# Regrouping four of eight MLP input tiles by 32x32 block transposes and DRAM instead of transposing them on TensorE

## The chip, the core and the metric

One NeuronCore of a Trainium2 chip runs the whole layer. The metric is the device time of one execution in microseconds; the median of several runs is given. The engines work side by side, each through its own instructions in order: PE (TensorE), ACT (ScalarE), DVE (VectorE), POOL (GpSimd, here a DMA queue and a few elementwise operations) and SP (a DMA queue). They wait for each other at semaphores.

## What is computed

One layer of a streaming encoder on x of 1024 tokens by 1024 channels, in float32. A token-mixing part runs three branches (windowed attention, a state-space layer, cross-attention), gates and merges them; what follows it is the part that matters here:

```python
x = x + rmsnorm(merged @ w_out, g_mix_post)
h = rmsnorm(x, g_mlp_pre)
f = square(relu(h @ w_up)) @ w_down        # w_up 1024x4096, w_down 4096x1024
x = x + rmsnorm(f, g_mlp_post)
```

Tokens are cut into eight tiles of 128. The kernel keeps float32 accuracy by splitting every operand of a product into a high part (float32r, made by ScalarE) and a low part (the rest, made by VectorE) and adding three products: high-high, high-low and low-high.

## The kernel before, in words

The stage around the change goes through the eight tiles in an order written out by hand, `OUT_ORDER` (L50): `w0 w1 w2 h0 w3 h1 w4 h2 w5 h3 w6 h4 w7 h5`, and then `h6 h7` between the first MLP products. A `w` is the output projection of a tile, an `h` the turning of a tile of the MLP input h from tokens-by-channels into channels-by-tokens, the layout that the MLP's products need. All engines walk through the same order. For a tile t:

- TensorE, `w_out` (L2442): 24 matmuls of 512 columns into each of two banks, through the helper at L2146. For tiles 0 and 1 these are laid out differently, ahead of the loop.
- ScalarE copies both banks into `acc[t]` (L889), squares them and sums (`square_o`, L1145), and does the same for the residual of the tile before (`square_x`).
- VectorE, `residual` (L1826): scales the projection by the gain (L1831), makes 1/sqrt of the mean square in eight small steps (`rstd`, L1357 to L1363), multiplies and adds x (L1835). Then `h2` of the tile before (L1838): rstd again, and L1844 writes the normalised tile into one of two slots of `tok`. From the third tile on it first waits until TensorE has turned the tile that had the slot.
- TensorE, `h2_transposes` (L2450): eight 128x128 transposes (L2156) of a slot into two banks. ScalarE's `h2_hi` (L1150) takes the high part from the banks into `hThi` (L1154), VectorE's `h2_lo` (L1847) the low part into `hTlo` (L1852).
- POOL (loop at L808): waits for the residual of the tile, stores it (x1, L810), waits until the store has landed and h2 has been made, and loads x of the tile after the next (`x_load`, L798). There are two slots for x, `yx`.

Before the first MLP product TensorE waits until the parts of tiles 0 to 3 have been taken out of the banks, and in `plain_mlp`, before the fifth product, for those of tiles 4 to 7. The first product also needs the split weights of its unit; VectorE makes their low parts (`prep_lo`, L388) at the step `w7`, behind `h4`. Each `w` and each `h` takes the next two of the eight banks, in the order of `OUT_ORDER` (`out_event`, L134).

The kernel turns other things by blocks already: in the attention branches VectorE transposes 128x1024 tiles in 32x32 blocks (L1520, L1601), POOL stores the blocks to DRAM and brings them back regrouped with four loads of 128 KB per tile (L686, L713).

Of the kernel before, what the change touches and what calls it, by code (L numbers as in the profile page):

```python
# [16 lines left out]
P = 128  # L17
D = 1024
L = 1024
# [28 lines left out]
          ("glu", 16), ("mergeM", 16), ("mergeS", 16), ("out", 28), ("upA", 4), ("mlp", 192)]  # L48

OUT_ORDER = ["w0", "w1", "w2", "h0", "w3", "h1", "w4", "h2", "w5", "h3", "w6", "h4", "w7", "h5", "h6", "h7"]  # L50
FIRST = {}
_n = 0
for _name, _count in STAGES:
# [80 lines left out]
def out_event(kind, t, e):  # L134
    if kind == "h" and t > 5:
        return FIRST["upA"] + 2 + 3 * (t - 6) + e
    return FIRST["out"] + 2 * OUT_ORDER.index(f"{kind}{t}") + e

# [10 lines left out]
def hybrid_layer(nc, a, out):  # L149
# [4 lines left out]
    with ctx:  # L154
# [101 lines left out]

        craw = yst2.rearrange("p h (r d x) -> p h r d x", r=RP, d=2)
        x_blocks = [t1, t2]
        blocks = pT[:, :, :, :].rearrange("p a b c -> p a (b c)")
        prob_of = lambda q: prob[:, 2 * q:2 * q + 2, :].rearrange("p e c -> p (e c)")  # L260
        y_slots = [yst2[:, 0, :], yst2[:, 1, :]] + [xs[:, h, :, :].rearrange("p r n -> p (r n)") for h in range(2)]
# [21 lines left out]

        p_dram = nc.dram_tensor("prob_scratch", (16, P, L), f32, kind="Internal").ap()
        x_dram = nc.dram_tensor("x_blocks_scratch", (4, P, 2, 512), f32, kind="Internal").ap()
        y_dram = nc.dram_tensor("y_scratch", (2, BT, P, L), f32, kind="Internal").ap()
        g_dram = nc.dram_tensor("gate_scratch", (3, KT, P, L), f32, kind="Internal").ap()
        x1_dram = nc.dram_tensor("x1_scratch", (2, P, D), f32, kind="Internal").ap()
# [24 lines left out]
        turned, rope_done = sem("turned"), sem("rope_done")  # L313
        y_sent = [sem(f"y_sent{s}") for s in range(4)]
        x_turned, x_out, x_back_in = sem("x_turned"), sem("x_out"), sem("x_back_in")
        blocks_turned, blocks_out, p_back = sem("blocks_turned"), [sem(f"blocks_out{s}") for s in range(2)], sem("p_back")
        g_sent = [sem(f"g_sent{s}") for s in range(2)]
        gate_in = [sem(f"gate_in{s}") for s in range(4)]
# [331 lines left out]
        def _(pool):  # L650
# [157 lines left out]
            for t in range(NT):  # L808
                pool.wait_ge(x1_made, t + 1)
                g.dma_start(x1_dram[t - tile_of(NT - 2)] if tile_of(t) > 5 else out_rows[t], yx[:, t % 2, :]).then_inc(x1_sent, 16)  # L810
                if t + 2 < NT:
                    pool.wait_ge(x1_sent, 16 * (t + 1))
                    pool.wait_ge(h2_made, t + 1)
                    x_load(t + 2)
            g.memset(acc[:, :, :], 0.0).then_inc(acc_zero, 1)
            pool.wait_ge(h2_made, NT)
            for e in range(2):
# [65 lines left out]
        def _(act):  # L883
# [264 lines left out]
                square2("o", acc[:, t, :], 10 + t)  # L1148

            def h2_hi(t):  # L1150
                for e in range(2):
                    n = out_event("h", t, e)
                    wait_full(act, n)
                    A.activation(hThi[:, 4 * e:4 * e + 4, t * P:(t + 1) * P],  # L1154
                                 banks[n % 8][:, :].rearrange("p (k t) -> p k t", k=4), ACT.Copy).then_inc(split_hi, 1)
# [182 lines left out]
        def _(dve):  # L1338
# [487 lines left out]
            def residual(t):  # L1826
                for e in range(2):
                    wait_taken(dve, out_event("w", t, e))

                scaled = acc[:, (t + 4) % NT, :]  # L1830
                mark(V.tensor_tensor(scaled, acc[:, t, :], tok[:, 0:D], mul))  # L1831
                dve.wait_ge(sq_o, t + 1)
                rstd(sumsq[:, 10 + t:11 + t])
                dve.wait_ge(x_back[t % 2], 16 * (t // 2 + 1))
                V.scalar_tensor_tensor(out=yx[:, t % 2, :], in0=scaled, scalar=stat[:, 1:2], in1=yx[:, t % 2, :], op0=mul, op1=add)\  # L1835
                    .then_inc(x1_made, 1)

            def h2(t):  # L1838
                dve.wait_ge(sq_x, t + 1)
                if t >= 2:  # L1840
                    wait_full(dve, out_event("h", t - 2, 0))
                    wait_full(dve, out_event("h", t - 2, 1))
                rstd(sumsq[:, 18 + t:19 + t])
                V.scalar_tensor_tensor(out=tok[:, (2 + t % 2) * D:(3 + t % 2) * D], in0=yx[:, t % 2, :], scalar=stat[:, 1:2],  # L1844
                                       in1=tok[:, D:2 * D], op0=mul, op1=mul).then_inc(h2_made, 1)

            def h2_lo(t):  # L1847
                for e in range(2):
                    n = out_event("h", t, e)
                    sl = (slice(None), slice(4 * e, 4 * e + 4), slice(t * P, (t + 1) * P))  # L1850
# [286 lines left out]
        def _(pe):  # L2137
# [317 lines left out]

            for step in OUT_ORDER[:-2]:
                t = int(step[1])
                if step[0] == "h":
                    h2_transposes(t)
                    continue  # L2460
                for e in range(2 if t > 1 else 0):
                    w_out(t, e)

            for t in range(4):
                for e in range(2):
                    wait_taken(pe, out_event("h", t, e))


            def plain_mlp():
                for pc, (s, cc, hf) in enumerate(UP_FIRST):  # L2470
# [1 line left out]
                    if pc in (2, 3):  # L2472
                        h2_transposes(pc + 4)
                    if pc == 4:
                        for t in range(4, NT):
                            for e in range(2):
                                wait_taken(pe, out_event("h", t, e))
                    unit(u)
# [109 lines left out]
```

## Time and profile before

| | us |
|---|---|
| median of three runs | 1439.28 |
| lowest and highest run | 1438.74, 1439.55 |
| the profiled execution | 1438.89 |
| its span, first to last instruction | 1436.9 |
| TensorE busy in the span | 1422.6 (99%) |
| VectorE busy | 1047.4 (73%) |
| ScalarE busy | 514.9 (36%) |
| POOL busy | 241.7 (17%) |

The profile is one execution on the chip. A row of a timeline gives the start in us from the beginning of the span, the duration in us, the engine, the line of the kernel, the operation, what it writes and reads, and in brackets how long the engine had been idle and what released it. Matmuls are pipelined, so that their durations overlap; the distance of their starts is their pace. For a DMA the duration is that of its issue, and the time to landing runs from the issue to the semaphore that tells that the data is there.

### The profile page before, as it was taken

The page shows a single profiled execution, that of the slowest core. Times are in us where ns is not written, and L with a number is a line of the kernel's source. Part 1 is how long each engine was busy: PE and PEld are TensorE (multiplying, and loading weights), DVE is VectorE, ACT ScalarE, POOL GpSimd, SP SyncE. Part 2 cuts the span into 40 slices and gives each one's busy share as a digit, 9 for nine tenths or more (in the row PEclk, how much of TensorE's full clock was granted, in tenths as well). Part 3 has the DMA queues.
Part 4 walks back from the last instruction along what each step waited for, and adds up shares of the span by engine and source line. Part 5 has one row for each costly group of instructions (what it writes and reads, how often), then busy time and mean ns, then how long its engine had stood idle before and what let it go on. Part 6 is the DMA issues. An engine that isn't in the chain of part 4 may idle for free.

```text
span 1436.9 us, 18375 instructions
## 1 busy us (share of the span) xinstructions
PE 1422.6 (99%) x6998; PEld 1178.1 (82%) x6998; DVE 1047.4 (73%) x1718; ACT 514.9 (36%) x637; POOL 241.7 (17%) x392
## 2 busy tenths in 40 slices
PE   8999999999999999999999999999999999999997
PEld 7888688878888888888888888888888888888886
DVE  6769768964854526456766779797979796979887
ACT  4445653131211352311333432333334333434334
POOL 0003313431111131001000304211010102020112
PEclk9999999999999999999999999999999999999999
DMA  9306525954234387234433447936363737364546
GB/s 337 74 30 190 166 85 175 275 195 149 71 106 139 93 272 256 93 96 151 162 104 89 133 146 228 299 118 203 119 203 117 234 94 239 105 203 143 160 152 117
DMA packets 136241, 227.04 MB, mean 158 GB/s; under 512 B 23048, under 2 KB 74288, under 8 KB 136176
## 3 DMA queue, kind: packets, MB, share of 16 engines
q0 software_dynamic: 52960, 139.24, 31.2%
q1 hardware_dynamic: 83200, 86.92, 19.1%
q8 instruction: 42, 0.69, 0.2%
q14 instruction: 23, 0.19, 0.0%
q10 hardware_dynamic: 16, 0.00, 0.0%
HBM read 175.53 MB, written 50.59 MB: 157 GB/s over the span
## 4 chain that ended last, share of the span: by engine, by line
PE 94%; DVE 3%; DMA 1%; issue 1%; ACT 0%; DVEq 0%; SPq 0%; ACTq 0%
PE bank L2146 55%; PE bank L2515 17%; PE bank L2535 15%; PE bank L2186 1%; PE bank L2156 1%; PE bank L2248 1%; PE bank L2268 1%; DMA raw<-in_w_down_dram 1%; PE bank L2375 1%; PE bank L2380 1%; PE bank L2284 1%; PE bank L2345 1%; PE bank L2330 1%; DMA xst<-in_mem_dram 0%; DVE wlo L388 0%
## 5 line engine op out<-in xcount | busy, mean ns | idle before, releaser
L2146 PE MATMUL bank<-hThi,whi 128*128 128x512 f32 x800 | 313.9, 392 | 0.1
L2146 PE MATMUL bank<-hThi,wlo 128*128 128x512 f32 x800 | 311.4, 389 | 0.0
L2146 PE MATMUL bank<-hTlo,whi 128*128 128x512 f32 x800 | 311.4, 389 | 0.0
L2146 PEld LDWEIGHTS bank<-hThi,whi 128*128 128x128 f32 x800 | 150.2, 188 | 32.2 <-issue 1.2
L2146 PEld LDWEIGHTS bank<-hThi,wlo 128*128 128x128 f32 x800 | 150.2, 188 | 31.6
L2146 PEld LDWEIGHTS bank<-hTlo,whi 128*128 128x128 f32 x800 | 150.2, 188 | 30.7
L1212 ACT ACTIVATE whi<-raw 128x1024 fp32r<-128x1024 f32 x91 | 95.3, 1055 | 182.3 <-DVE raw L1953 97.6
L1943 DVE TENSOR_TENSOR wlo<-raw,whi 128x1024 fp32r<-128x1024 f32 x91 | 110.9, 1219 | 34.4 <-ACT whi L1212 34.4
L2535 PE MATMUL bank<-whi,yhi 128*128 128x512 f32 x336 | 130.8, 389 | 0.6 <-DVE acc L1976 0.6
L2535 PE MATMUL bank<-wlo,yhi 128*128 128x512 f32 x336 | 130.7, 389 | 0.0
L2515 PE MATMUL bank<-hThi,whi 128*128 128x512 f32 x336 | 130.7, 389 | 0.0
L2515 PE MATMUL bank<-hTlo,whi 128*128 128x512 f32 x336 | 130.7, 389 | 0.0
L2515 PE MATMUL bank<-hThi,wlo 128*128 128x512 f32 x336 | 130.7, 389 | 0.0
L2535 PE MATMUL bank<-whi,ylo 128*128 128x512 f32 x336 | 130.7, 389 | 0.0
L388 DVE TENSOR_TENSOR wlo<-raw,whi 128x2048 fp32r<-128x2048 f32 x33 | 75.2, 2280 | 57.4 <-ACT whi L382 57.1
L382 ACT ACTIVATE whi<-raw 128x2048 fp32r<-128x2048 f32 x32 | 61.1, 1911 | 79.7 <-PE bank L2146 51.8
L1019 ACT ACTIVATE scr<-bank 128x512 f32<-128x512 f32 x48 | 28.5, 597 | 162.9 <-PE bank L2146 133.6
L1976 DVE TENSOR_TENSOR acc<-bank,acc 128x1024 f32<-128x1024 f32 x72 | 86.0, 1217 | 1.0 <-PE bank L2535 1.0
L2535 PEld LDWEIGHTS bank<-whi,yhi 128*128 128x128 f32 x336 | 63.1, 188 | 14.0 <-DVE acc L1976 1.0
L2535 PEld LDWEIGHTS bank<-whi,ylo 128*128 128x128 f32 x336 | 63.1, 188 | 13.2
L2515 PEld LDWEIGHTS bank<-hThi,wlo 128*128 128x128 f32 x336 | 63.1, 188 | 13.2
L2515 PEld LDWEIGHTS bank<-hThi,whi 128*128 128x128 f32 x336 | 63.1, 188 | 13.1
(398 smaller groups left out, 2568.7 us busy)
## 6 DMA issues: line engine op xcount, KB each, us to landing
hThi<-h_scratch POOLq DMA_DIRECT2D x42, 512.0 KB, 4.8
hTlo<-h_scratch POOLq DMA_DIRECT2D x42, 512.0 KB, 5.7
raw<-in_w_in_dram SPq DMA_DIRECT2D x34, 512.0 KB, 7.2
raw<-in_w_up_dram SPq DMA_DIRECT2D x32, 512.0 KB, 4.3
raw<-in_w_down_dram SPq DMA_DIRECT2D x32, 512.0 KB, 4.6
gate_scratch<-scr POOLq DMA_DIRECT2D x48, 256.0 KB, 3.1
tok<-gate_scratch POOLq DMA_DIRECT2D x24, 512.0 KB, 4.2
prob_scratch<-pT POOLq DMA_DIRECT2D x16, 512.0 KB, 3.5
```

Source lines behind the costliest of these rows:

```text
L382: nc.scalar.activation(parts(u)[0], raw[:, u % 2, :], ACT.Copy).then_inc(w_hi, 1)
L388: nc.vector.tensor_tensor(lo, raw[:, u % 2, :], hi.bitcast(f32), sub).then_inc(w_lo, 1)
L1019: A.activation(scr[:, gp % 2, :], banks[n % 8][:, :], ACT.Sigmoid).then_inc(bank_free[n % 8], 1)
L1212: A.activation(w_slot(whi, place), source, ACT.Copy).then_inc(w_hi, 1)
L1943: V.tensor_tensor(w_slot(wlo, place), source, w_slot(whi, place).bitcast(f32), sub).then_inc(w_lo, 1)
L1976: V.tensor_tensor(dst[:, 2 * h:2 * h + 2, :], pair_banks(k), dst[:, 2 * h:2 * h + 2, :], add).then_inc(pair_free[k], 1)
L2146: ins = T.matmul(dst, lhs(k)[p], rhs(k)[q], start=start and k == 0 and i == 0, stop=stop and k == kt - 1 and i == 2)
L2156: ins = T.transpose(banks[n % 8][:, i * P:i * P + P] if dsts is None else dsts[i], src, by)
L2186: ins = T.matmul(banks[n % 8][:, 0:256], wk[:, c] if s < 2 else memT[:, k, c], memT[:, k, :] if s < 2 else wk, start=k == 0, stop=k == KT - 1)
L2248: ins = T.matmul(banks[n % 8][:, hh * 256:hh * 256 + 256], tokq[:, h, (e // 2) * P:(e // 2 + 1) * P], kmT[:, h, :], start=True, stop=True)
L2515: ins = T.matmul(banks[2 * k + c][:, :], w[:, kk, c * P:c * P + P], x[:, kk, :], start=opens and kk == 0 and i == 0, stop=kk == 3 and i == ...
L2535: ins = T.matmul(banks[2 * k + t % 2][:, :], x[:, kk, rows], w[:, kk, :], start=opens and kk == 0 and i == 0, stop=kk == 1 and i == 2, ski ...
```

## The change

For tiles 0 to 3 (`HB = 4`) TensorE no longer transposes h. VectorE, behind `h2`, transposes the slot in 32x32 blocks into `acc[t]`. POOL, at the end of its turn for that tile, waits for this, stores the blocks to a new DRAM tensor, waits for the store to land, and brings them back with four loads into the same slot of `tok`. ScalarE waits for these loads and makes the high parts out of the slot, with a rearranged reading order, VectorE the low parts. `h2` of tiles 2 to 5 waits for VectorE's own low parts instead of TensorE's transposes, the residual of tiles 4 to 7 for the landing of a block store, since it writes where the blocks lay. The four `h` steps leave the sequence of banks. Before the first MLP product TensorE waits for eight counts of the new semaphore `h_parts`. Tiles 4 to 7 are as before. The core of the diff:

```diff
-          ("glu", 16), ("mergeM", 16), ("mergeS", 16), ("out", 28), ("upA", 4), ("mlp", 192)]
+          ("glu", 16), ("mergeM", 16), ("mergeS", 16), ("out", 20), ("upA", 4), ("mlp", 192)]
...
+HB = 4
+OUT_EVENTS = [w for w in OUT_ORDER if w[0] == "w" or int(w[1]) >= HB]
...
-    return FIRST["out"] + 2 * OUT_ORDER.index(f"{kind}{t}") + e
+    return FIRST["out"] + 2 * OUT_EVENTS.index(f"{kind}{t}") + e
...
+        h2_slot = lambda t: tok[:, (2 + t % 2) * D:(3 + t % 2) * D]
...
+        hb_dram = nc.dram_tensor("h2_blocks_scratch", (HB, P, L), f32, kind="Internal").ap()
...
                     x_load(t + 2)
+                if t < HB:
+                    pool.wait_ge(blocks_turned, 16 + t + 1)
+                    g.dma_start(hb_dram[t], acc[:, t, :]).then_inc(blocks_out[t % 2], 16)
+                    pool.wait_ge(blocks_out[t % 2], 128 + 0 * (1 - t % 2) + 16 * (t // 2 + 1))
+                    src = hb_dram[t].rearrange("(a s) (b x) -> b s a x", a=4, b=4)
+                    for b in range(4):
+                        g.dma_start(h2_slot(t)[32 * b:32 * b + 32, :].rearrange("s (a x) -> s a x", a=4), src[b]).then_inc(xp_back[t % 2], 16)
...
             def h2_hi(t):
+                if t < HB:
+                    act.wait_ge(xp_back[t % 2], 16 * 16 + 64 * (t // 2 + 1))
+                    for e in range(2):
+                        A.activation(hThi[:, 4 * e:4 * e + 4, t * P:(t + 1) * P].rearrange("p k (a r) -> p k a r", a=4),
+                                     h2_slot(t).rearrange("p (a k r) -> p k a r", a=4, k=KT)[:, 4 * e:4 * e + 4], ACT.Copy).then_inc(split_hi, 1)
+                    return
...
                 scaled = acc[:, (t + 4) % NT, :]
+                if 4 <= t < HB + 4:
+                    dve.wait_ge(blocks_out[t % 2], 128 + 0 * (1 - t % 2) + 16 * (t // 2 - 1))
...
                 dve.wait_ge(sq_x, t + 1)
-                if t >= 2:
+                if 2 <= t < HB + 2:
+                    dve.wait_ge(h_parts, 2 * (t - 1))
+                elif t >= 2:
...
                                        in1=tok[:, D:2 * D], op0=mul, op1=mul).then_inc(h2_made, 1)
+                if t < HB:
+                    dve.wait_ge(h2_made, t + 1)
+                    V.transpose(acc[:, t, :].rearrange("p (b k r) -> p k b r", b=4, k=KT),
+                                h2_slot(t).rearrange("p (k b s) -> p k b s", k=KT, b=4)).then_inc(blocks_turned, 1)

             def h2_lo(t):
+                if t < HB:
+                    for e in range(2):
+                        by_block = lambda y: y[:, 4 * e:4 * e + 4, t * P:(t + 1) * P].rearrange("p k (a r) -> p k a r", a=4)
+                        dve.wait_ge(split_hi, 20 + 2 * t + e + 1)
+                        V.tensor_tensor(by_block(hTlo), h2_slot(t).rearrange("p (a k r) -> p k a r", a=4, k=KT)[:, 4 * e:4 * e + 4],
+                                        by_block(hThi).bitcast(f32), sub).then_inc(h_parts, 1)
+                    return
...
                 if step[0] == "h":
-                    h2_transposes(t)
+                    if t >= HB:
+                        h2_transposes(t)
                     continue
...
-            for t in range(4):
-                for e in range(2):
-                    wait_taken(pe, out_event("h", t, e))
+            pe.wait_ge(h_parts, 8)
```

## Rows read from the trace of the kernel before

**Rows 1.** The page, the chain that ended last, its shares by engine.

```profile
PE 94%; DVE 3%; DMA 1%; issue 1%; ACT 0%; DVEq 0%; SPq 0%; ACTq 0%
```

**Rows 2.** The chain's pieces in time (start, us), then TensorE's timeline at tiles 4 and 5.

```profile
739.72 0.87 PE bank L2156 x8
740.59 10.90 PE bank L2146 x48
...
786.65 0.60 PE L2156 MATMUL bank<-ident,tok 128*128 128x128 f32 x4
...
799.21 0.48 PE L2146 MATMUL bank<-hThi,whi 128*128 128x512 f32 x1
```

**Rows 3.** VectorE's timeline: h2, residual, rstd, residual's end, next rstd, low parts, weights.

```profile
736.72 1.28 DVE L1844 SCALAR_TENSOR_TENSOR tok<-yst,stat,tok 128x1024 f32<-128x1024 f32 x1
740.45 1.23 DVE L1831 TENSOR_TENSOR acc<-acc,tok 128x1024 f32<-128x1024 f32 x1 [2.45 <-ACT acc L889]
741.62 0.15 DVE L1357 TENSOR_SCALAR stat<-sumsq 128x1 f32<-128x1 f32 x1
...
743.40 1.28 DVE L1835 SCALAR_TENSOR_TENSOR yst<-acc,stat,yst 128x1024 f32<-128x1024 f32 x1
744.61 0.15 DVE L1357 TENSOR_SCALAR stat<-sumsq 128x1 f32<-128x1 f32 x1
...
...
794.68 1.28 DVE L1852 TENSOR_TENSOR hTlo<-bank,hThi 128x512 fp32r<-128x512 f32 x2
795.88 4.48 DVE L388 TENSOR_TENSOR wlo<-raw,whi 128x2048 fp32r<-128x2048 f32 x2
```

**Rows 4.** Line 1520, the block transpose of attention: count, ns min/median/max, first and last start.

```profile
L1520 DVE STREAM_TRANSPOSE pT<-prob x8: 1245/1246/1248, 115.2 to 149.6; 128x1024 f32<-128x1024 f32 x8
```

**Rows 5.** ScalarE's timeline, a half tile copied from SBUF.

```profile
812.27 0.63 ACT L1202 ACTIVATE yhi<-yst 128x512 fp32r<-128x512 f32 x1 [5.93 <-DVE yst L1909]
```

**Rows 6.** POOL's timeline, x loads of tiles 3 and 6 and an x1 store.

```profile
748.22 0.53 POOL L798 DMA_DIRECT2D yst<-in_x_dram  x1 [8.60 <-DVE tok L1844]
748.79 0.54 POOL L810 DMA_DIRECT2D x_scratch<-yst  x1
...
783.56 0.53 POOL L798 DMA_DIRECT2D yst<-in_x_dram  x1 [10.65 <-DVE tok L1844]
```

**Rows 7.** POOL in attention: a block store, its landing; four loads behind it, theirs.

```profile
151.19 0.56 POOL L690 DMA_DIRECT2D prob_scratch<-pT  x1 [1.56 <-DVE pT L1520]
...
DMA to landing us min/median/max: 4.8/4.8/4.8
...
156.23 2.18 POOL L686 DMA_DIRECT2D prob<-prob_scratch  x4 [2.30 <-DMA prob_scratch<-pT]
...
DMA to landing us min/median/max: 2.8/5.0/6.5
```

**Rows 8.** Line 810, the six x1 stores between 738 and 797 us, landing.

```profile
DMA to landing us min/median/max: 5.1/5.4/6.8
```

**Rows 9.** Line 810, the x1 store at 731.2 us, landing.

```profile
DMA to landing us min/median/max: 2.9/2.9/2.9
```

**Rows 10.** Landings: line 678 at 303.1 us; line 840's two stores at 850.9; line 734 at 300.9.

```profile
DMA to landing us min/median/max: 4.3/4.3/4.3
...
DMA to landing us min/median/max: 2.9/3.3/3.7
...
DMA to landing us min/median/max: 2.8/2.9/2.9
```

**Rows 11.** Line 798, the six x loads between 738 and 797 us, landing.

```profile
DMA to landing us min/median/max: 4.4/4.6/6.4
```

**Rows 12.** Two tiles of the stage: busy by engine, granted clock, DMA share, GB/s.

```profile
740.45:752.23 11.78, 11.78 (x59) 9.84 (x58) 7.85 (x24) 4.48 (x9) 1.07 (x2) 1.00 0.46 139
752.23:764.00 11.77, 11.77 (x59) 9.83 (x58) 7.84 (x23) 4.47 (x9) 1.06 (x2) 1.00 0.32 91
```

**Rows 13.** The core's span and mean granted clock.

```profile
core 0: 1436.9 us, clock 0.998
```

More of the change, by code:

```diff
@@ L315, in hybrid_layer @@
         x_turned, x_out, x_back_in = sem("x_turned"), sem("x_out"), sem("x_back_in")
+        h_parts = sem("h_parts")
         blocks_turned, blocks_out, p_back = sem("blocks_turned"), [sem(f"blocks_out{s}") for s in range(2)], sem("p_back")
@@ L2474, in plain_mlp @@
                     if pc == 4:
-                        for t in range(4, NT):
+                        if HB > 4:
+                            pe.wait_ge(h_parts, 2 * HB)
+                        for t in range(HB, NT):
                             for e in range(2):
```

## Prediction

> **What bounds the kernel now.** I read the chain that ended last first: TensorE carries 94% of it, no other engine more than 3% [rows 1]. Whatever TensorE is spared, and whatever it is made to wait, goes to the end. Then I read the stage that the diff touches, engine by engine: the output projection and the transposes of the MLP input, from 728 to 817 us. TensorE's pieces of the chain follow each other there without a gap [rows 2]: eight transposes, 0.87 us, then a tile's projection, 48 matmuls in 10.90. Four of eight tiles lose their transposes: 4 x 0.87 = **3.48 us** is all that can be gained, and TensorE's pace becomes 10.90 us a tile where it was 11.77.
>
> The sum is made against the profiled execution: 1438.89 us, a span of 1436.9 and 1.99 around it. The median of the runs is 1439.28, 0.39 above; the difference that I find is added to the median.
>
> **The change part by part.** *VectorE.* A tile now takes 1.17 + 1.78 + 1.21 us for the residual, the same 1.78 + 1.21 for h2 and 1.20 for the low parts [rows 3], 8.35 together. A block transpose of this very shape takes 1.25 [rows 4]; for its wait on the h2 just written I allow 0.1, since the 1.78 of rstd hold eight small steps that wait for each other like that. Low parts read from SBUF instead of PSUM: at the pace of elements either way, nothing. That is 9.7 us in a tile of 10.90: hidden as long as no input is late; if one is, all of it queues behind.
>
> *ScalarE* reads eight halves from SBUF, 0.63 us each [rows 5], beside TensorE: nothing. But it now waits in order until a tile is back from DRAM, with the copies of the next projection behind that wait, and VectorE's residual behind them.
>
> *TensorE* gives up its waits for those banks and gets one for the parts, and the projections have four pairs of banks to themselves: nothing.
>
> *POOL* is the place that decides. Today it issues, per tile, one load of x and one store of x1, back to back, and waits only for VectorE [rows 6]. After the change its loop runs in one line: the x1 store, **wait until it has landed**, x load, block store, **wait until it has landed**, four loads, and only then the next x1 store. (The first of these waits exists today, but the wait for h2 covers it.) So a circle of POOL is: landing of the x1 store + 0.25 + x load issue 0.53 + landing of the block store + 0.25 + four issues 2.2. The 0.25 is from landing to the next issue: a store of 151.19 lands after 4.8, at 156.0, and POOL goes on at 156.23; four loads of the shape wanted here take 2.2 to issue [rows 7].
>
> The landings: the block store stands directly behind an x load, as the x1 store does today. Six of those take 5.1 to 6.8, median 5.4 [rows 8]; the only one with nothing ahead takes 2.9 [rows 9]. I take **5.3**, between shortest and median, since the 6.8 came once. The x1 store will stand behind four loads of 128 KB, which no row shows at this size. Below: the lone store, 2.9. Above: the store behind an x load, 5.4. Between: a store of half the size directly behind four such loads took 4.3, beside other traffic, and the second of two full stores issued together 3.7 [rows 10]. I take **3.7**: the four loads leave at the pace of their issue, 0.55 us each, and so fill the queue hardly more than one store does.
>
> The circle is then 3.7 + 0.25 + 0.53 + 5.3 + 0.25 + 2.2 = **12.23 us**, more than TensorE's 10.90. What is late is the x load that the residual needs. In time: h2 of tile 0 is made at 738.0 [rows 3] and transposed at 739.35, its store starts 0.3 later at 739.65 (so long after the last transpose starts the store in rows 4 and 7), lands at 744.95, and the loads are issued from 745.2 to 747.4. There the x1 store of tile 1 starts, and a circle apart the x loads of tiles 3, 4, 5 and 6: 751.35, 763.6, 775.8 and 788.05 (today the first goes at 748.22, the last at 783.56 [rows 6]). They land after 4.6 [rows 11].
> - x of tile 5 is there at 780.4; the residual's last step, 1.21, and h2, 2.99, give h2(4) at 784.65. TensorE wants it after projection 6, whose end is now at 786.65 [rows 2] and comes 3.48 earlier, 783.15: a pause of 1.5.
> - TensorE goes on: 784.7 + 0.87 + 10.90 = 796.45. x of tile 6 is there at 792.65, h2(5) at 796.9: pause 0.45.
> - The first MLP product needs low parts of its weights, which VectorE makes in 2.24 behind h2(5) and 1.2 us of low parts [rows 3]: 796.9 + 1.2 + 2.24 + 0.1 = 800.4. Today it starts at 799.21 [rows 2].
>
> So the 3.48 us are paid back and 1.2 more: 1439.28 + 1.2 = **1440.5 us**. The blocks' own way back is just covered: if the loads land in 2.9, as a pass with nothing ahead of it did [rows 10], tile 1's parts leave VectorE waiting for x of tile 4 some 0.6 us; at the 4.0 of busier passes, which I count in the range, it costs about half a microsecond. Each 0.1 us of either landing is worth 0.4 at the end, since four circles stand one behind the other; so the ends lie far apart.
>
> **The rivals.** *A: the full gain, 1435.8 us.* If both stores land like a lone store or one behind a store (2.9 to 3.7), the circle is 9.0 to 10.6 us and fits into 10.90; nothing pauses and 3.48 us stay. For it: the DMA engines are busy 46% and 32% of a tile in this stage [rows 12]. Against it: every store behind an x load took 5.1 or more, in this very stage. The Trainium skill ("DMA: Bandwidth & Descriptors", section on the anatomy of one DMA on the gpsimd path) fits 2.0 us plus the bytes over 436 GB/s, by my estimate 3.2 us for each store; by that rule this case would come about. The lone row (2.9) agrees with it, the rows behind an x load don't.
>
> *B: slower, 1442.9 to 1446.9 us.* The x1 store behind the four loads lands in 4.3 (the half-size row) to 5.3 (like the one behind an x load): four times 0.6 to 1.6 us more than the sum has. It decides from 4.1 us on, where the time passes +0.2%. For it: the only row with that very order; against it: that row had other traffic beside it.
>
> *C: slower, about 1443.5 us.* The last of the four loads lands after 6.5 us, as in the pass of rows 7: tile 2 is back at 777.8 instead of 774.2; ScalarE's two parts and two copies (some 2.6), the residual (4.2) and h2 (3.0) then end at 787.6, 3.0 us behind the sum. Against it: nothing else uses the queues in this stage.
>
> *D: about 1443.4 us.* The granted clock is 1.00 in this stage [rows 12] and 0.998 over the span [rows 13]; no row shows what a pause in the middle does to it. All that the clock cost in this execution is 0.002 x 1436.9 = 2.9 us, and that is my price on top of the sum. The Trainium skill ("TensorE: Matmul & The Clock Gate", Part 1) has the clock fall from 2.4 to 1.2 GHz when the engine idles and rise again under work; no run here shows it in mid-kernel.
>
> That the change removes no TensorE time can be left out: the transposes stand on the chain [rows 2].
>
> **How the numbers follow.** No change that can be told (0.2%, 2.9 us, is about what a measurement of this kernel can tell): the sum and its surroundings, 0.42. A: 0.20. B 0.23, C 0.10 and D 0.05 are slower: 0.38. The range goes from A's floor to the upper part of B: 1435.5 to 1445.5. The likeliest case's own range is 1436.4 to 1442.2.
>
> **What would show it.** In the trace after: 32 transposes of h2 on TensorE instead of 64; POOL's x1 stores of tiles 1 to 4 some 12.2 us apart, the x loads of tiles 5 and 6 at about 775.8 and 788; a pause of TensorE ahead of the transposes of tile 4, released by VectorE's h2, and one ahead of the first MLP product. I am wrong if those stores are 10.9 us apart and nothing pauses (A), if a block store behind an x load lands in about 3 us, if a projection waits for banks, or if ScalarE's wait for the blocks ends later than the x load (C).

## The result, and the profile after

The changed kernel takes **1444.05 us** (median of 7 runs, 1442.63 to 1447.91) against 1439.28 for the kernel before beside it (7 runs, 1438.11 to 1440.51): a ratio of 1.0037, 95% interval 1.0025 to 1.0049. It is slower by 4.8 us where the prediction had 1.2: inside its range, above the likeliest case's own (1436.4 to 1442.2). The profiled execution took 1444.53 us, with a span 5.7 us longer than that of [rows 13].

The core's span and clock, then the waits of TensorE in the changed kernel: engine, tile and line, what was waited for; us in total, times, longest.

```profile
core 0: 1442.6 us, clock 0.997
...
PE bank L2189 <- DVE tok L1866: 2.9, 2, 2.6
PE bank L2179 <- issue: 2.4, 1, 2.4
PE bank L2549 <- DMA hTlo<-h_scratch: 1.8, 1, 1.8
```

The first two are new and stand in the stage that was changed; the third stands 115 us later, in the MLP. The chain of the page no longer helps: its shares (below, to be read beside [rows 1]) add up to 38%, so it does not reach back to the stage.

```profile
PE 35%; DMA 1%; DVE 1%; POOL 1%; issue 0%; ACT 0%; DVEq 0%; POOLq 0%
```

POOL's timeline in the stage, the turns of tiles 1 to 4, to be read beside [rows 6]: start, us, line, what is issued, and in brackets the idle time before it.

```profile
747.25 0.57 POOL L815 DMA_DIRECT2D out_dram<-yst  x1
751.06 0.56 POOL L803 DMA_DIRECT2D yst<-in_x_dram  x1 [3.24 <-DMA out_dram<-yst]
751.61 0.53 POOL L822 DMA_DIRECT2D h_blocks_scratch<-acc  x1
758.62 2.22 POOL L826 DMA_DIRECT2D tok<-h_blocks_scratch  x4 [6.48 <-DMA h_blocks_scratch<-acc]
760.83 0.56 POOL L815 DMA_DIRECT2D x_scratch<-yst  x1
765.57 0.56 POOL L803 DMA_DIRECT2D yst<-in_x_dram  x1 [4.17 <-issue]
766.12 0.53 POOL L822 DMA_DIRECT2D h_blocks_scratch<-acc  x1
771.55 2.22 POOL L826 DMA_DIRECT2D tok<-h_blocks_scratch  x4 [4.89 <-DMA h_blocks_scratch<-acc]
773.76 0.56 POOL L815 DMA_DIRECT2D x_scratch<-yst  x1
777.46 0.56 POOL L803 DMA_DIRECT2D yst<-in_x_dram  x1 [3.13 <-DMA x_scratch<-yst]
778.01 0.53 POOL L822 DMA_DIRECT2D h_blocks_scratch<-acc  x1
783.59 2.22 POOL L826 DMA_DIRECT2D tok<-h_blocks_scratch  x4 [5.04 <-DMA h_blocks_scratch<-acc]
785.80 0.56 POOL L815 DMA_DIRECT2D out_dram<-yst  x1
789.57 0.56 POOL L803 DMA_DIRECT2D yst<-in_x_dram  x1 [3.21 <-DMA out_dram<-yst]
```

The turn is the line of work that was foretold. From x1 store to x1 store it takes 13.58, 12.93 and 12.04 us (forecast 12.23), and the x loads leave at 751.06, 765.57, 777.46 and 789.57 (forecast 751.35, 763.6, 775.8 and 788.05). Two of the turns are long for reasons of their own: the block store of tile 1 landed after 6.7 us, and in the next turn POOL sat 4.17 us where the store of x1 had landed after 3.5.

Landings of the x1 stores of tiles 1 to 4, of the block stores, of the four loads, and of the x loads in this stage, to be read beside [rows 7, 8, 10, 11].

```profile
DMA to landing us min/median/max: 3.4/3.5/3.5
...
DMA to landing us min/median/max: 4.6/5.2/6.7
...
DMA to landing us min/median/max: 2.8/2.9/3.0
...
DMA to landing us min/median/max: 4.3/4.6/6.0
```

VectorE's steps that TensorE waits for, the last the low parts of the MLP's first weights, with the block transpose of the same profile [rows 3, 4], then ScalarE's copies from the slots, grouped [rows 5].

```profile
L1870 DVE STREAM_TRANSPOSE acc<-tok x4: 1245/1246/1247, 738.6 to 774.4; 128x1024 f32<-128x1024 f32 x4
...
782.10 1.29 DVE L1855 SCALAR_TENSOR_TENSOR yst<-acc,stat,yst 128x1024 f32<-128x1024 f32 x1 [0.89 <-DMA yst<-in_x_dram]
785.08 1.28 DVE L1866 SCALAR_TENSOR_TENSOR tok<-yst,stat,tok 128x1024 f32<-128x1024 f32 x1
...
799.74 4.48 DVE L393 TENSOR_TENSOR wlo<-raw,whi 128x2048 fp32r<-128x2048 f32 x2
...
L1166 ACT ACTIVATE hThi<-tok 128x512 fp32r<-128x512 f32 x8 | 4.6, 624 | 31.0 <-DMA tok<-h_blocks_scratch 31.0
```

The residual of tile 5 waits for its x, and h2(4) comes out at 786.3 instead of 784.65. TensorE's timeline at the three pauses shows it, to be read beside [rows 2]:

```profile
786.41 1.09 PE L2189 MATMUL bank<-ident,tok 128*128 128x128 f32 x8 [2.64 <-DVE tok L1866]
...
798.68 1.09 PE L2189 MATMUL bank<-ident,tok 128*128 128x128 f32 x8 [0.23 <-DVE tok L1866]
...
802.12 0.77 PE L2179 MATMUL bank<-hThi,whi 128*128 128x512 f32 x1 [2.35 <-issue]
```

TensorE stood 2.64, 0.23 and 2.35 us: 5.22, where 3.48 had been taken from it (32 transposes of h2 are left in the stage, where the kernel before has 64). The profile gives no releaser for the third pause; it ends when the first half of the weights' low parts is made, at 799.74 + 2.24. And the first MLP product, at 802.12, takes 0.77 for its first matmul where [rows 2] have 0.48. Busy time by engine, granted clock (0.50 is 1.2 GHz, 1.00 is 2.4 GHz), DMA share and GB/s there, to be read beside [rows 12]:

```profile
786.00:788.00 2.00, 1.59 (x11) 1.50 (x12) 0.36 (x1) 0.00 (x0) 0.36 (x1) 1.00 0.93 307
802.00:804.00 2.00, 1.88 (x5) 1.52 (x6) 2.00 (x2) 0.51 (x2) 0.00 (x0) 0.50 0.96 378
804.00:806.00 2.00, 2.00 (x7) 1.58 (x6) 1.90 (x7) 0.00 (x0) 0.00 (x0) 0.66 1.00 350
```

The clock stayed up behind the pause of 2.64 us and fell behind that of 2.35. The 5.7 us of the span then divide at three marks. TensorE would have begun the transposes of tile 4 at 786.41 - 2.64 = 783.77 without the pause; in the execution before it was 786.65, or 783.17 less the 3.48. So 0.6 us are older than any pause. Up to the first product, 12.56 us in the execution before, it now takes 802.12 - 783.77 = 18.35: 5.8 us, the pauses of 5.22 and some tenths in which the engine runs dry and fills again. From there to the end it is 640.5 us where it was 637.7: 1.2 of these 2.8 are the longer wait in the MLP (1.8 us where there was one of 0.6), and **1.6** are left for the clock. -3.48 + 0.6 + 5.8 + 1.2 + 1.6 = 5.7.

### The profile page after: what moved, and what is told of

It is laid out like the page before. It is cut to its first block and busy times, and to the rows that moved or that the text cites. A ratio compares the mean times of both kernels' runs of the same rounds, so it can differ in the third digit from the quotient of the medians.

```text
span 1442.6 us, 18327 instructions
## 1 busy us (share of the span) xinstructions
PE 1421.9 (99%) x6966; PEld 1176.0 (82%) x6966; DVE 1053.2 (73%) x1722; ACT 514.6 (36%) x637; POOL 253.0 (18%) x412
## 5 line engine op out<-in xcount | busy, mean ns | idle before, releaser
L2569 PEld LDWEIGHTS bank<-whi,ylo 128*128 128x128 f32 x336 | 63.1, 188 | 13.1
L2549 PEld LDWEIGHTS bank<-hThi,wlo 128*128 128x128 f32 x336 | 63.1, 188 | 13.1
```

The source lines that it names most:

```text
L2549: ins = T.matmul(banks[2 * k + c][:, :], w[:, kk, c * P:c * P + P], x[:, kk, :], start=opens and kk == 0 and i == 0, stop=kk == 3 and i == ...
L2569: ins = T.matmul(banks[2 * k + t % 2][:, :], x[:, kk, rows], w[:, kk, :], start=opens and kk == 0 and i == 0, stop=kk == 1 and i == 2, ski ...
```

## The experiments

The theory: POOL's turn is what puts the loads of x late, and so makes the pauses; the clock and the later wait come on top. The kernel before was run beside each of three groups of kernels, each group on one chip: 1439.15 us beside the store first, the x loads on SP and the first row of runs with TensorE kept awake; 1439.59 beside the blocks on SP, the dose, the first repetition of the change and the six tiles; 1439.54 beside the doubled dose, the second repetition and the second row with TensorE kept awake.

### The turn made shorter

**The block store ahead of the wait for the x1 store.** The two landings then run side by side.

```diff
+                if t < HB:
+                    pool.wait_ge(blocks_turned, 16 + t + 1)
+                    g.dma_start(hb_dram[t], acc[:, t, :]).then_inc(blocks_out[t % 2], 16)
                 if t + 2 < NT:
                     pool.wait_ge(x1_sent, 16 * (t + 1))
                     pool.wait_ge(h2_made, t + 1)
                     x_load(t + 2)
                 if t < HB:
-                    pool.wait_ge(blocks_turned, 16 + t + 1)
-                    g.dma_start(hb_dram[t], acc[:, t, :]).then_inc(blocks_out[t % 2], 16)
                     pool.wait_ge(blocks_out[t % 2], 128 + 0 * (1 - t % 2) + 16 * (t // 2 + 1))
```

> POOL issues the block store ahead of the x load instead of behind it; everything else is as in the changed kernel. Theory P (POOL's circle of two in-line waits makes the x loads late): the block store now stands behind the x1 store alone and lands in some 3.5 to 3.7 us instead of 5.1 to 6.7, both waits overlap, the circle falls from about 12.9 us to 7 to 10, the x loads follow VectorE again, TensorE's pause ahead of the transposes of tile 4 (2.6 us) and ahead of the first MLP product (2.35) shrink to 1 us or less together, and the clock stays at 1.00: 1435.8 to 1437.5 us. Rival S (the blocks' round trip in front of ScalarE's in-order wait ends last): the trip is only 1 to 2 us shorter, the copies of the projections still wait behind it, pauses of 2 us or more stay: 1440 to 1443.

Measured: 1439.98 us, ratio 1.0003 (0.9994 to 1.0012): between the theory and the rival, and nearer to the rival's number. The x loads leave at 751.42, 763.44, 774.53 and 785.35, the last 4.2 us earlier than with the change, and the pauses shrink to 0.82 and 1.03 us. Order alone gives back some 4 us, and the granted clock is 1.00 from 783 to 808. Why the pauses do not go altogether is in POOL's rows; the landings of the four block stores stand behind them:

```profile
773.98 0.56 POOL L818 DMA_DIRECT2D h_blocks_scratch<-acc  x1 [5.12 <-DVE acc L1871]
774.53 0.54 POOL L803 DMA_DIRECT2D yst<-in_x_dram  x1
...
DMA to landing us min/median/max: 2.9/2.9/3.9
```

The x load now stands behind the block store, and with it behind the wait for VectorE's block transpose: the x1 store of this turn had landed at 772.3 (768.31 and 4.0), and the x load left at 774.53. VectorE still waited for x last, 1.1 to 2.5 us in each of tiles 4 to 6, and not for ScalarE, as the rival had it. The block store took 2.9 us, with the x load issued behind it instead of ahead of it.

**The x loads on SP's queue**, which has nothing to do in this stage; POOL is left with the x1 store and the way of the blocks.

```diff
+            yx_sp = yst[:, :, :].rearrange("p (s a) c -> p s (a c)", s=2)
...
+                if s == 1:
+                    for t in range(NT - 2):
+                        sp.wait_ge(x1_sent, 16 * (t + 1))
+                        sp.wait_ge(h2_made, t + 1)
+                        sp.dma_start(yx_sp[:, t % 2, :], x[t + 2]).then_inc(s_in[t % 2], 16)
...
-                if t + 2 < NT:
+                if t >= HB and t + 2 < NT:
                     pool.wait_ge(x1_sent, 16 * (t + 1))
-                    pool.wait_ge(h2_made, t + 1)
-                    x_load(t + 2)
...
-                dve.wait_ge(x_back[t % 2], 16 * (t // 2 + 1))
+                dve.wait_ge((x_back if t < 2 else s_in)[t % 2], 16 * (t // 2 + 1))
```

> The x loads of tiles 2 to 7 are issued by SP's queue with the same waits; POOL keeps the x1 stores and the blocks. Theory P: POOL's circle loses the x load and the wait for the x1 store (x1 store issue 0.56, block store landing 3.7 to 5.3, 0.25, four issues 2.2: 7 to 8.5 us, below TensorE's 10.9), x is there in time, no pause above 1 us, 1435.8 to 1437.5 us. Rival S: the blocks come back no earlier relative to h2, ScalarE's wait stays, 1440 to 1443.

Measured: 1437.53 us, ratio 0.9992 (0.998 to 1.0004), an interval that still holds 1. No pause is left in the stage: the first product starts at 795.80, 3.41 us before that of [rows 2], which is the saving. From there on 2.38 us go into one wait for the MLP's loads, as in the changed kernel:

```profile
912.00 0.50 PE L2553 MATMUL bank<-hThi,whi 128*128 128x512 f32 x1 [2.38 <-DMA hTlo<-h_scratch]
```

**The blocks on SP's queue instead**, x loads and x1 stores on POOL as before the change.

```diff
+                if s == 1:
+                    for t in range(HB):
+                        sp.wait_ge(blocks_turned, 16 + t + 1)
+                        sp.dma_start(hb_dram[t], acc[:, t, :]).then_inc(s_in[t % 2], 16)
+                        sp.wait_ge(s_in[t % 2], 16 + 16 * (t // 2 + 1))
+                        back = hb_dram[t].rearrange("(a s) (b x) -> b s a x", a=4, b=4)
+                        for b in range(4):
+                            sp.dma_start(tok[32 * b:32 * b + 32, (2 + t % 2) * D:(3 + t % 2) * D].rearrange("s (a x) -> s a x", a=4), back[b]).then_inc(s_in[2 + t % 2], 16)
...
-                if t < HB:
-                    pool.wait_ge(blocks_turned, 16 + t + 1)
...
```

> The block stores and the four loads of each tile go out on SP's queue (other semaphores, nothing else changed), so POOL's turn is again x1 store, its landing, x load. Theory (POOL's circle is what puts the loads of x late): x loads 10.9 to 11.0 us apart, no pause of TensorE over 0.5 us in the stage, the first product at 795.5 to 796.5 us after the start, 1435.5 to 1438 us. Rival (the transfers themselves are in each other's way, 16 DMA engines for all queues): x1 stores and x loads land as late as with the change, pauses of 1 us or more stay, 1440 us or more. A third (SP's queue brings the blocks back later, since each of its four loads is issued behind the other and the weights' loads stand behind them): ACT waits over 10 us for a tile, and the pause is ahead of the first product.

Measured: **1436.54 us, ratio 0.9979 (0.9971 to 0.9988)**: faster than the kernel before by 3.05 of the 3.48 us. SP's queue and POOL's in the stage:

```profile
749.92 0.34 SPq L633 DMA_DIRECT2D h_blocks_scratch<-acc  x1
755.79 1.77 SPq L637 DMA_DIRECT2D tok<-h_blocks_scratch  x4
...
760.85 0.53 POOL L811 DMA_DIRECT2D yst<-in_x_dram  x1 [10.59 <-DVE tok L1867]
770.93 0.53 POOL L811 DMA_DIRECT2D yst<-in_x_dram  x1 [9.01 <-DVE tok L1867]
782.32 0.53 POOL L811 DMA_DIRECT2D yst<-in_x_dram  x1 [10.27 <-DVE tok L1867]
```

POOL waits for VectorE again, as in [rows 6], not for landings, and TensorE has no pause before the first product at 796.59. The transfers are the same as with the change, and the stores land no faster (5.4 to 6.6 us for the x1 stores, 5.7 to 6.6 from a block store's issue to that of its loads), so it was neither their volume nor their landing that cost the time, but that all of them were waited for in one line. VectorE and ScalarE have the same work as with the change, too.

### The turn made longer

**A dose of four small memsets** on POOL behind the four loads, each waited for.

```diff
                         g.dma_start(h2_slot(t)[32 * b:32 * b + 32, :].rearrange("s (a x) -> s a x", a=4), src[b]).then_inc(xp_back[t % 2], 16)
+                    for i in range(4):
+                        g.memset(den[:, :], 0.0).then_inc(skip_zero, 1)
+                        pool.wait_ge(skip_zero, 1 + 4 * t + i + 1)
```

> A dose: four small POOL memsets of a tile that nothing reads any more, each waited for, behind the four loads of tiles 0 to 3: about 0.8 us more in POOL's turn, four times. Theory (POOL's circle paces the x loads, and nothing takes the delay up): x loads of tiles 3, 4, 5 and 6 later by 0.8, 1.6, 2.4 and 3.2 us than with the change, the first product about 3 us later, 1446 to 1448 us. Rival (something else is last, VectorE or the transfers, and POOL has room): same as the change within 1 us.

Measured: 1444.32 us (1442.85 to 1449.48), ratio 1.0038 (1.0023 to 1.0052): no more than the changed kernel beside it (1445.51). That was a miss, and by its number the rival's case. In its profiled execution (1448.67 us, among the longest of the eight) the dose is there, 1.17 us a turn, but some of it is taken up again: with the memsets between them the x1 store no longer stands right behind the four loads, and lands in 2.9 us instead of 3.5. POOL waits 2.65 us for it and not 3.13:

```profile
775.60 0.80 POOL L828 MEMSET den<- 128x64 f32 x4
776.76 0.56 POOL L815 DMA_DIRECT2D x_scratch<-yst  x1 [0.36 <-POOL den L828]
779.96 0.56 POOL L803 DMA_DIRECT2D yst<-in_x_dram  x1 [2.65 <-DMA x_scratch<-yst]
```

What is left is some 0.5 us a turn (against the mark explained below the x load of tile 6 is 1.9 us later than in a repetition of the change, 792.70 - 786.01 for 788.66 - 783.89), no more than what one execution of the changed kernel differs from the next. So it was doubled (`range(8)`, 2.0 us a turn in the trace; the expectation has 2.3, and its 3.2 and 3.7 us for the x1 store run to POOL's next issue).

> The dose doubled: eight memsets with their waits, 2.3 us in POOL's turn (the four took 1.17 with the waits, and 0.5 of that was taken up, because the x1 store no longer stood behind the four loads and landed in 3.2 instead of 3.7 us; the time did not rise). Theory (POOL's circle paces the x loads; what the store saves by standing alone is used up at some 0.5 to 0.8 us a turn): 1.5 to 1.8 us more in each of four turns than with the change, the x load of tile 6 5 to 7 us later, 1449 to 1453 us. Rival (POOL has room, and something else paces): within 1.5 us of the change.

Measured: 1448.88 us (1447.90 to 1450.38), ratio 1.0061 (1.0048 to 1.0074), 3.4 us above the changed kernel beside it (1445.52): just under what the theory had, and outside the rival's 1.5. Single runs of the two overlap (1447.90 to 1450.38 beside 1442.88 to 1449.81); against all 18 runs of the changed kernel (median 1445.13) the difference is 3.7. The x load of tile 6 leaves 10.9 us after TensorE reached the end of projection 6 (796.64 and 792.11 - 6.33 = 785.78); in the first repetition of the changed kernel, below, it was 4.8 (788.66 and 783.89). It is 6.1 us later, in the 5 to 7 foretold. TensorE:

```profile
792.11 1.97 PE L2192 MATMUL bank<-ident,tok 128*128 128x128 f32 x8 [6.33 <-DVE tok L1869]
...
808.93 0.47 PE L2182 MATMUL bank<-hThi,whi 128*128 128x512 f32 x1 [1.19 <-issue]
```

The pause grew where the theory puts it, ahead of the transposes of tile 4. The clock fell behind that pause (0.50 and 0.51 from 792 to 798) and not, as in the changed kernel's profile, behind the last one, so part of the 3.4 us is the clock's.

### The changed kernel again, and the clock

**The changed kernel, repeated** in two further rows of runs.

> The changed kernel itself, once more, in the same row of runs as the three that follow. Theory (the pauses of 2.6, 0.2 and 2.4 us come out of POOL's circle, which takes about 12.9 us where TensorE's turn takes 10.9): they come again, tiles 4 to 6 are loaded 3 to 5 us later than in the kernel with the x loads on SP's queue, and the time is 1443 to 1445 us, 4 us above the kernel before. Rival (the one profiled execution had a slow x load and a slow block store, 6.0 and 6.7 us, by chance, and these made the delay): circles of 12.2 us or less, a pause of 1.5 us or less ahead of the first product, and 1440 to 1441.5 us.

> The changed kernel a third time, on the same chip as the two that follow, so that the kernel with TensorE kept awake is compared with it side by side. Both theories expect 1443 to 1446 us and again pauses of 4 to 5.5 us together in the stage, and the clock at half ahead of or in the first MLP product.

Measured: 1445.51 us, ratio 1.0036 (1.0023 to 1.0049), and 1445.52, ratio 1.0045 (1.0029 to 1.0061). The pauses come again, 1.67 and 2.35 us in the first, 1.61, 0.23 and 2.35 in the second; the x loads of the first leave at 750.90, 764.38, 776.63 and 788.66, within 0.9 us of the forecast. Without the slow block store of the first profile (6.7 us; 5.7 and 5.8 at most here) the pause ahead of tile 4 is 1 us shorter, no more. The clock, though, is not the same from one execution to the next. In the second repetition it fell neither in this stage nor behind it, against what was expected (it had fallen 10 us into the span, behind a wait for the first weights); in the first it fell twice, behind 2.35 us in the stage and again behind the wait in the MLP. The row of granted clock behind the last pause in the second repetition (the number before the last two), then TensorE's timeline at the wait in the MLP in the first:

```profile
804.00:806.00 2.00, 1.86 (x8) 1.59 (x9) 2.00 (x2) 0.55 (x2) 0.00 (x0) 1.00 0.97 386
...
918.62 0.79 PE L2549 MATMUL bank<-hThi,whi 128*128 128x512 f32 x1 [2.38 <-DMA hTlo<-h_scratch]
919.22 0.63 PE L2549 MATMUL bank<-hTlo,whi 128*128 128x512 f32 x1
919.64 0.63 PE L2549 MATMUL bank<-hThi,wlo 128*128 128x512 f32 x1
...
921.74 0.40 PE L2549 MATMUL bank<-hTlo,whi 128*128 128x512 f32 x1
921.97 0.40 PE L2549 MATMUL bank<-hThi,wlo 128*128 128x512 f32 x1
```

A matmul each 0.42 us, and from 921.74 on each 0.23. The granted clock is 0.57 from 918 to 920, 0.58 from 920 to 922, and 1.00 behind.

**TensorE kept awake**: ten products that are thrown away, into the bank of the first MLP product, ahead of it.

```diff
             pe.wait_ge(h_parts, 8)
+            wait_free(pe, up_event(0, True))
+            for _ in range(10):
+                T.matmul(banks[up_event(0, True) % 8][:, :], yhi[:, 0, 0:P], yhi[:, 0, 0:512], start=True, stop=True)
```

> The changed kernel, but TensorE fills its pause ahead of the first MLP product with ten matmuls (2.3 us) into the bank of that product, whose result is thrown away. If the lower clock behind that pause (0.50 and 0.66 granted from 802 to 806 us) comes from the pause and costs what it seems to, 1.6 to 1.9 us: 1442.2 us, clock 1.00 throughout. If the earlier pause or something else lowers the clock: 1444.0, and the clock still falls.

> The ten products that are thrown away ahead of the first MLP product, again. What is disputed is the price of the clock: the trace of the change shows 12 matmuls at 0.427 us instead of 0.227, less than 2.5 us and by the sum 1.7; the first time the gain was 3.5 us, but against runs of another chip. Theory (the clock alone, 1.7 us): 1.7 us below the change beside it. Rival (the drop costs more than its own matmuls, since the work behind it falls in with other transfers): 3 us or more below it.

Measured: 1440.51 us, ratio 1.0009 (1.0000 to 1.0019), 1.7 below what the first expectation had, and 1440.76, ratio 1.0011 (1.0002 to 1.0021), 4.76 us below the changed kernel beside it (1445.52): by size the rival's 3 us or more. Its reason, that the fall brings the later waits with it, does not hold: the wait in the MLP comes in profiles without a fall behind the first product, too (table). The 12 slow matmuls of the second expectation are some eight in the trace of the change, 802.12 to 805.25, at 0.2 us each the same 1.6. The first profile of it, TensorE ahead of the first product and the clock behind:

```profile
798.04 2.57 PE L2501 MATMUL bank<-yhi 128*128 128x512 f32 x10
800.59 0.50 PE L2179 MATMUL bank<-hThi,whi 128*128 128x512 f32 x1
...
802.00:806.00 4.00, 4.00 (x20) 3.30 (x19) 3.72 (x12) 0.00 (x0) 0.00 (x0) 1.00 0.96 348
```

The ten products fill the last pause and the clock holds; the pause ahead of tile 4 stays (1.33 and 1.66 us). The profiles of all executions, divided at the same marks, show where the rest is (in us; "mark" is where the transposes of tile 4 would have begun without the pause ahead of them):

| kernel | mark | pauses up to the first product | first product | clock fell after | wait in the MLP | first product to the end |
|---|---|---|---|---|---|---|
| before | 786.65 | none | 799.21 | - | 0.6 | 637.7 |
| change | 783.77 | 2.64, 0.23, 2.35 | 802.12 | the third | 1.8 | 640.5 |
| change again | 783.89 | 1.67, 2.35 | 800.94 | the second; 2.38 in the MLP | 2.4 | 642.7 |
| change beside kept awake | 786.83 | 1.61, 0.23, 2.35 | 804.14 | - | 1.7 | 638.9 |
| store first | 783.06 | 0.82, 1.03 | 797.82 | - | 2.0 | 639.1 |
| x loads on SP | 783.24 | none | 795.80 | - | 2.4 | 639.7 |
| blocks on SP | 784.03 | none | 796.59 | - | 0.8 | 637.9 |
| kept awake | 783.81 | 1.33 | 800.59 | - | 0.4 | 637.6 |
| kept awake again | 783.02 | 1.66 | 800.18 | - | none | 637.3 |
| dose | 786.01 | 2.98, 1.93 | 805.30 | both | 2.4 | 641.3 |
| dose doubled | 785.78 | 6.33, 1.19 | 808.93 | the first | 2.3 | 639.4 |

In the rows without a fall behind the first product, the last column less the wait in the MLP is 637.1 to 637.3. So everything behind the first product is that wait and the clock: 640.5 - 637.1 - 1.8 = 1.6 us for the one fall of the change, 642.7 - 637.1 - 2.4 = 3.2 for the two of its repetition, 641.3 - 637.1 - 2.4 = 1.8 with the dose. With the two doses the clock fell ahead of the first product, too: from the transposes of tile 4 to the first product, less the pauses between, it is 15.6 us with the doubled dose, 14.4 with the dose and 13.0 to 13.1 with the change. So a fall costs 1.3 to 2.5 us in these profiles.

Three profiles say little of how often the clock falls, but the mean granted clock of every run is known: 0.9963 over the 18 runs of the change, 0.9982 over 71 of the kernel before, 0.9979 over the 23 with TensorE kept awake. Each value is given to 0.001, or 1.4 us, so what follows is an estimate from the means: (0.9982 - 0.9963) x 1444 is some 2.7 us a run for the change, and 2.3 of the 4.76 us go to the clock.

The wait in the MLP is 1.7 to 2.4 us in all three profiles of the change, and with TensorE kept awake it does not come (the 0.4 in the table is a wait for VectorE, as is the 0.6 of the kernel before). That makes up most of the rest of the 4.76 as far as two profiles can say. **Why it goes is open.** In every profile without a fall behind the first product and with four tiles, the load that TensorE waits for, the last of a row on POOL's queue, is issued 98.4 to 98.6 us after the first product, and SP's weights 104.5 us after it; only the landing differs, with the DMA queues full (380 GB/s and more): 14.4 to 15.7 us before, with blocks on SP and with TensorE kept awake, 16.8 to 17.7 in the others.

### Six tiles

**Tiles 4 and 5 by blocks too**, on top of the x loads on SP's queue; their PSUM banks are handed on empty.

```diff
-HB = 4
+HB = 6
...
-                    if t >= HB:
-                        h2_transposes(t)
+                    if t >= 4:
+                        for e in range(2):
+                            wait_free(pe, out_event("h", t, e))
+                            pe.sem_inc(bank_full[out_event("h", t, e) % 8], 1)
```

> The x loads on SP's queue as before, and tiles 4 and 5 by blocks through DRAM too (their transposes on TensorE left out; the PSUM banks are handed on empty). Theory (with POOL's circle cut short, each tile that leaves TensorE is worth its 0.87 us): 1.74 us less than the kernel with the x loads on SP and four tiles, which was at 1437.5: 1435 to 1436.5 us, a few us below the kernel before. Rival (the way through DRAM is too long at the end of the stage, ACT waits for tile 5's blocks and does the square of tile 7 and the first rectifier late): TensorE waits for tile 7's h2 or for the first bank, 1437.5 us or more.

Measured: 1441.24 us (1438.51 to 1444.87), ratio 1.0008 (0.9997 to 1.0018), where four tiles had 1437.53 and 0.9992 in their own row of runs. The two intervals overlap, so the times alone do not decide it; the profile does. The rival held, one engine further on than it said:

```profile
796.07 4.49 DVE L393 TENSOR_TENSOR wlo<-raw,whi 128x2048 fp32r<-128x2048 f32 x2 [1.51 <-ACT whi L387]
...
798.46 0.77 PE L2186 MATMUL bank<-hThi,whi 128*128 128x512 f32 x1 [4.57 <-issue]
```

ScalarE waited up to 6.5 us for a tile's blocks with the copies of the MLP's weights queued behind, VectorE's low parts of them came 1.5 us late behind that, and TensorE stood 4.57 us and went on at half clock. Tile 4's blocks were back at 792.60, and the last projection ended at 798.46 - 4.57 = 793.89: at the end of the stage there is no projection left to cover the way through DRAM.

## Why the prediction was right, and what it missed

- **That TensorE bounds the stage and 3.48 us can be gained:** right. With the blocks on SP's queue 3.05 us were left in the medians, and the first product came 2.6 to 3.4 us earlier in the two profiles without pauses.
- **That POOL's turn takes it back:** right, and shown from both sides: shorter turns remove the pauses, longer ones (doubled dose) lengthen them. Its terms: x1 store 3.4 to 3.5 us (taken 3.7), block store 5.2 in the median (taken 5.3), four issues 2.22 (2.2), landing to next issue 0.25 (0.25). Turns of 12.04 where nothing came between (12.23); the other two had 1.4 us of a slow store and 1.0 us in which POOL stood for nothing that the profile shows.
- **The three waits:** in place and kind as foretold, ahead of tile 4, of tile 5 and of the first product. Taken 1.5 and 0.45, and by its own numbers 800.4 - 796.9 - 0.87 = 2.6 ahead of the first product; 2.64, 0.23 and 2.35 in the first profile, 1.67, none and 2.35 in the second, 1.61, 0.23 and 2.35 in the third. From the end of projection 6 to the first product that made 800.4 - 783.15 = 17.25 us; it took 18.35, 17.05 and 17.31.
- **VectorE, ScalarE, the loads back:** right (1.246 us a block transpose, 0.624 a half, 2.8 to 3.0 us a landing). ScalarE waited 31.0 us for blocks in four tiles, and none of it was last.
- **Rival A fell by the block stores:** 4.6 to 6.7 us where it needed 3.7 or less, so that on one queue the turn is 12 us and more. Its price was nearly right for a change that was not made, the one with two queues (1436.54 for 1435.8). The Trainium skill's fit ("DMA: Bandwidth & Descriptors", section on the anatomy of one DMA on the gpsimd path; 3.2 us by my estimate) holds for the x1 stores (3.4 to 3.5, and 2.9 behind a dose) and not for the block stores behind an x load (4.6 to 6.7). What was issued just ahead of it goes with the difference, on either queue: the same store took 2.9 with the x load issued behind it (store first), 7.2 when SP issued an x load at the same moment and 3.3 to 3.7 in the other three turns (x loads on SP), and 5.7 to 6.6 on SP's queue just behind POOL's x load and x1 store (blocks on SP).
- **B and C fell, though the time is theirs:** 1444.05 lies in B's range and near C's 1443.5, but the x1 stores took 3.4 to 3.5 us and not 4.3 or more, and the last of the four loads landed after 3.0 at most, not 6.5. The range reached as far as it did for B's sake; that it holds the measured time, which came about in another way, is luck. And the ratio is clear of the 0.2% under which the prediction spoke of no change that can be told (0.42): what came is a slower kernel (0.38).
- **What failed is the end of the sum.** "So the 3.48 us are paid back and 1.2 more" stops at the first MLP product, and takes all behind it as unchanged. Behind it another 2.8 us came in the first profile: the clock, which was rival D at 0.05 and priced with 2.9, and 1.2 us of a wait in the MLP that the text doesn't have. D is no rival but a part of the likeliest case: it came in two of three profiles of the change, once or twice, 1.6 us each, and makes some 2.7 us a run by the estimate above. That its price of 2.9 is so near is luck as well: the 0.002 it was taken from cost nothing, since they lie at the end of the span, where TensorE has no work left. In the kernel before its last matmul starts at 1427.7, the granted clock is 1.00 up to 1432 us, 0.59 from there to 1434, and then:

```profile
1434.00:1436.90 2.90, 0.00 (x0) 0.00 (x0) 0.44 (x1) 0.00 (x0) 0.00 (x0) 0.50 0.47 181
```

  That it should fall behind a pause is what the Trainium skill says ("TensorE: Matmul & The Clock Gate", Part 1); that it did so behind some pauses and not behind others of the same length is in the runs.
- The row "0.6 us older than any pause" is a difference between executions. The mark lies between 783.0 and 786.8 in the ten that have the four tiles alone; in the latest of them, 2.4 us are a wait for the very first weights, behind which the clock fell as well.

## What to carry to other kernels

Write a queue's loop as a circle, landing by landing, and hold it against the pace of the bounding engine; where it is longer, give one of the two ways to a queue that idles before giving up the change: the same transfers on two queues turned +4.8 us into -3. When the bounding engine is going to pause for some 2 us (the shortest pause with a fall behind it was 1.93 here), put the clock into the sum with a price per fall (here 1.3 to 2.5 us). And a way with a long latency pays only as long as there is work behind it to cover it: four tiles did, six did not.

## What the hardware showed beyond that

The clock fell to half behind pauses of 1.93, 2.35, 2.38, 2.98, 4.57 and 6.33 us, and stayed at 1.00 behind others of 2.64, 2.35 (second repetition of the change) and 2.38 (x loads on SP): the length of the pause alone does not decide.

POOL issued the x load of tile 4 some 0.9 to 1.0 us later than the landing of the x1 store ahead of it allows (idle 4.17, 4.13 and 4.03 us in the three profiles of the change, where the turns beside it have 3.1 to 3.3), always in this turn and still there with both doses (3.53 where the neighbours have 2.6 to 2.7). With the x loads on SP's queue it stands 0.80 us between the first and the second of tile 2's four loads instead, so it is not bound to that wait. What it did is not known.

SP takes 0.34 us to issue a block store and 1.75 for the four loads, POOL 0.53 and 2.22.
